# A two-layer model kernel on one core: gate sigmoids moved behind the softmax heads, norms four tiles at a time, and a re-ordered convolution

## The reference, cut to what matters

```
def conformer_conv(h, w_in, b_in, dw, dw_b, ln_g, ln_b, w_out, b_out):
    u = h @ w_in + b_in
    u = u[..., :D] * jax.nn.sigmoid(u[..., D:])
    u = causal_dwconv(u, dw) + dw_b            # 31 taps
    u = jax.nn.silu(layernorm(u, ln_g, ln_b))
    return u @ w_out + b_out

def hybrid_layer(...):
    h = rmsnorm_2(x, norm_mix_g)
    gq, gk, gv, gr, glr, fq, fk, fv, ff, g_gla, g_fox = jnp.split(h @ w_in, IN_OFFSETS, axis=-1)
    o_gla = gla_chunked(...)                   # 4 heads
    o_gla = rmsnorm_2(o_gla, ...) * jax.nn.silu(gr)
    fqh = rmsnorm_2(fq, ...); fkh = rmsnorm_2(fk, ...)
    o_fox = fox_attention(fqh, fkh, fv, log_f) # 8 heads, softmax
    y = jax.nn.sigmoid(g_gla + gate_b[0]) * (o_gla @ w_gla_branch) \
        + jax.nn.sigmoid(g_fox + gate_b[1]) * (o_fox @ w_fox_branch)
    x = x + y @ w_out
```

## Time and profile before

| what | us |
|---|---|
| median of 3 runs | 2668.36 (2668.05 to 2668.66) |
| the profiled execution | 2671.43 |
| its span, first to last instruction | 2669.6 |
| PE busy in the span | 2539.5 (95%) |
| DVE busy | 1345.3 (50%) |
| ACT busy | 1138.2 (43%) |
| POOL busy | 996.6 (37%) |

### The profile page before, as it was taken

One profiled execution on the slowest core, in us unless ns is written; L12 is line 12 of the kernel. 1 busy time (PEld: TensorE's weight loads), 2 busy tenths in 40 slices (PEclk: granted clock), 3 DMA queues, 4 the chain that ended last, 5 costly groups with the idle time before them and its releaser, 6 DMA issues.

```text
span 2669.6 us, 62382 instructions
## 1 busy us (share of the span) xinstructions
PE 2539.5 (95%) x25300; PEld 2385.7 (89%) x25300; DVE 1345.3 (50%) x2023; ACT 1138.2 (43%) x1656; POOL 996.6 (37%) x488
## 2 busy tenths in 40 slices
PE   7998998999999999998999999999998989999998
PEld 6787886997999999876979999999997659999998
DVE  7566555623477731897333777521162234455521
ACT  7844445543444333325433444332436432444422
POOL 3333220551444444334313444444332103444442
PEclk8899999999999999998999999999999899999999
DMA  4221001431222233223212222333221102222232
GB/s 144 79 64 49 1 3 64 142 131 40 90 91 92 90 112 126 81 67 119 79 48 81 93 93 92 107 103 110 86 88 56 32 0 80 95 94 94 94 103 72
DMA packets 62181, 219.44 MB, mean 82 GB/s; under 512 B 6752, under 2 KB 9184, under 8 KB 61408
## 3 DMA queue, kind: packets, MB, share of 16 engines
q1 hardware_dynamic: 58880, 207.76, 23.9%
q10 hardware_dynamic: 3168, 9.75, 1.0%
HBM read 213.29 MB, written 4.19 MB: 81 GB/s over the span
## 4 chain that ended last, share of the span: by engine, by line
PE 79%; DVE 9%; issue 7%; ACT 4%; POOL 2%; DMA 0%; DVEq 0%; POOLq 0%; ACTq 0%
PE psum L561 66%; DVE psum L2615 5%; PE psum L703 3%; PE psum L711 2%; POOL wl L510 2%; PE psum L1054 1%; PE psum L1011 1%; PE psum L1230 1%; PE psum L1229 1%; ACT wh L1356 1%; DVE psum L2205 0%; PE psum L1252 0%; DVE fox_max L2801 0%; PE psum L1264 0%; PE psum L673 0%
## 5 line engine op out<-in xcount | busy, mean ns | idle before, releaser
L510 POOL TENSOR_TENSOR wl<-raw,wh 128x1024 fp32r<-128x1024 f32 x388 | 950.5, 2459 | 1530.0 <-ACT wh L1356 1530.0
L561 PE MATMUL psum<-acth,wh 128*128 128x256 f32 x3792 | 764.9, 283 | 17.1 <-DVE actl L2211 6.5
L561 PE MATMUL psum<-actl,wh 128*128 128x256 f32 x3792 | 755.1, 281 | 0.0
L561 PE MATMUL psum<-acth,wl 128*128 128x256 f32 x3792 | 754.9, 280 | 0.0
L1356 ACT ACTIVATE wh<-raw 128x1024 fp32r<-128x1024 f32 x388 | 406.8, 1055 | 560.7 <-PE psum L561 545.8
L561 PEld LDWEIGHTS psum<-acth,wh 128*128 128x128 f32 x3792 | 583.9, 189 | 33.9 <-issue 26.5
L561 PEld LDWEIGHTS psum<-acth,wl 128*128 128x128 f32 x3792 | 583.0, 189 | 0.0
L561 PEld LDWEIGHTS psum<-actl,wh 128*128 128x128 f32 x3792 | 582.2, 189 | 0.0
L2545 DVE TENSOR_TENSOR cu<-psum,rstd 128x512 f32<-128x512 f32 x132 | 91.0, 690 | 241.8 <-PE psum L561 224.6
L561 PE MATMUL psum<-hidh,wl 128*128 128x256 f32 x1056 | 209.5, 276 | 0.0
L561 PE MATMUL psum<-hidh,wh 128*128 128x256 f32 x1056 | 209.4, 276 | 0.0
(11 more groups left out here) (434 smaller groups left out, 4094.2 us busy)
## 6 DMA issues: line engine op xcount, KB each, us to landing
raw<-in_weights SPq DMA_DIRECT2D x388, 512.0 KB, 3.4
xt<-in_x SPq DMA_DIRECT2D x4, 512.0 KB, 5.6
xt<-in_x ACTq DMA_DIRECT2D x1, 2048.0 KB, 9.0
out_x<-xt SPq DMA_DIRECT2D x6, 256.0 KB, 2.3
mem<-in_mem ACTq DMA_DIRECT2D x1, 1024.0 KB, 10.8
memn<-memh ACTq DMA_DIRECT2D x1, 1024.0 KB, 6.3
memn<-meml ACTq DMA_DIRECT2D x1, 1024.0 KB, 9.6
memh<-memn ACTq DMA_DIRECT2D x1, 1024.0 KB, 4.9
```

Source lines behind the costliest of these rows:

```text
L510: pool.tensor_tensor(wl[:, s, :], raw[:, s, :], wh[:, s, :].bitcast(F32), ALU.subtract).then_inc(split_done, 1)
L561: ins = pe.matmul(out[:, n:n + HALF], w, m[:, n:n + HALF], start=first and n == 0, stop=last and n + HALF >= out.shape[1])
```

## The change

In the convolution: `PETAPS` goes from 6 to 7; PE's taps go singly between the `cin` tiles; ACT loads the Sigmoid table ahead of the first sigmoid, which now comes before the diagonals; DVE runs the chains of tiles 5, 6 and 7 three abreast and then 6 and 7 together; the sum of squares goes from PE to DVE (eight adds into `rstd` and one matmul, `norm_total`), the four `kv1b` tiles stand together, the Ln table is loaded early, and two `weight_high` move behind the Silu loop.

In the hybrid: ACT's `gate(n)` only loads weights; all 16 sigmoids run in fox heads 5, 6 and 7; the fox norms go four tiles at a time, Ln and Exp in place in banks 4 to 7, where DVE reads them; gate tiles stand elsewhere between the norm sums, and `gate(10 + h)` comes right after gla head h. DVE's product with the gates waits for `gated`.

```
-PETAPS = 6
+PETAPS = 7
@@ PE, convolution
-                taps(2)
-                dense("cin", "norm_conv", acth, actl, units=4, skip=8)
-                taps(4)
-                dense("cin", "norm_conv", acth, actl, units=4, skip=12)
+                for k in range(2, 6):
+                    taps(k)
+                    for j in (4 + 2 * k, 5 + 2 * k):
+                        tile("cin", j, "norm_conv", acth, actl)
                 taps(6)
+                taps(7)
...
-                for j in range(2):
+                for j in range(4):
                     tile("kv1b", j, "norm_mem0", memh, meml, n=MEM)
-                norm_sum("ln")
-                for j in range(2, 4):
-                    tile("kv1b", j, "norm_mem0", memh, meml, n=MEM)
+                norm_total("ln")
@@ PE, hybrid
-                for j in range(0, 8, 2):
-                    fox_sum(j)
-                    fox_sum(j + 1)
-                    gate(5 + j // 2)
-                pe.wait_ge(frs_ready, 8)
+                fox_sum(0)
+                fox_sum(1)
+                gate(5)
+                fox_sum(2)
+                fox_sum(3)
+                gate(6)
+                gate(7)
+                for j in range(4, 8):
+                    fox_sum(j)
+                gate(8)
+                pe.wait_ge(fox_scaled, 5)
                 gla_scores(0)
                 gate(9)
+                pe.wait_ge(fox_scaled, 8)
                 for h in range(4):
                     gla_head(h)
+                    gate(10 + h)
                     if h < 3:
                         gla_scores(h + 1)
-                    gate(10 + h)
                     gla_sum(h)
@@ ACT, convolution
+                act.activation(tmp[:, 0, 0:1], b_eps, ACT.Sigmoid)
+                sigmoid(0)
+                weights(0)
                 diagonals(2)
...
+                act.activation(tmp[:, 0, 0:1], b_eps, ACT.Ln)
@@ ACT, hybrid
                 def gate(n):
-                    act.wait_ge(evacuated, t0 + 25 + n + 1 + UC)
-                    g_ = (gate_b if n // KT else gate_a)[:, n % KT, :]
-                    act.activation(g_, g_, ACT.Sigmoid, bias=pc("gate_b_2", n)).then_inc(gated, 1)
                     inner_high(25 + n, 26 + n)
+                def sigmoids(n0, n1):
+                    for n in range(n0, n1):
+                        g_ = (gate_b if n % 2 else gate_a)[:, n // 2, :]
+                        act.activation(g_, g_, ACT.Sigmoid, bias=pc("gate_b_2", n // 2 + KT * (n % 2))).then_inc(gated, 1)
...
                     act.activation(fpt[:, h % 2, 7 * P:10 * P], bank[2][:, 0:3 * P], ACT.Identity).then_inc(fpt_a, 1)
+                    if h == 7:
+                        sigmoids(12, 16)
...
+                    if h in (5, 6):
+                        act.wait_ge(evacuated, t0 + 41 + UC)
+                        sigmoids(6 * (h - 5), 6 * (h - 4))
@@ DVE, convolution
-                both(4, 11, 23, 6)
-                both(5, 17, 30, 12)
-                both(6, 18, 30, 13)
-                alone(7, 17, 12)
+                both(4, 13, 25, 7)
+                three(18, 30, 12)
+                both(6, 18, 18, 12)
...
+                for k in range(KT):
+                    if k + 2 < KT:
+                        centred(k + 2)
+                    dve.wait_ge(sq_ready, plan("ln", "sq") + k + 1)
+                    dve.wait_ge(sq_used, plan("ln", "sq") + k + SC)
+                    dve.tensor_tensor(rstd[:, :], rstd[:, :], sq[:, k % 2, :], add).then_inc(sq_used, 1)
```

More of the change, by code:

```diff
@@ L195, in build_program @@
             plan.take("kv1b", tile=4)
-            plan.take("ln", sq=KT, rstd=1, split=KT)
+            plan.take("ln", sq=KT, rstd=1, split=KT, total=1)
             plan.take("cout", tile=8, x=KT)
@@ L1069, in convolution, with taps @@
             def convolution():
[L1071 to L1081, removed]
+                def taps(k):
+                    pe.wait_ge(diag_ready, k - 1)
+                    pe.wait_ge(glu_ready, k + 1)
+                    if k >= 4:
+                        pe.wait_ge(u_ready, k - 3)
+                    for j in range(PETAPS):
+                        ins = pe.matmul(bank[4 + k % 4][:, :], diag[k % 2][:, j, :], gp[:, k, j:j + T],
+                                        start=(j == 0), stop=(j == PETAPS - 1))
+                    ins.then_inc(tap_mm, 1)
                 def mean(k0, k1):
@@ L1852, in gates, with weights, diagonals @@
                                    bias=pc("conv_b_in", k + KT)).then_inc(sig_ready, 1)
[L1854 to L1861, removed]
+                def weights(k):
+                    weight_high(UNIT0["cin"] + 2 * k + SLOTS)
+                    weight_high(UNIT0["cin"] + 2 * k + 1 + SLOTS)
+                def diagonals(k):
+                    if k >= 4:
+                        act.wait_ge(tap_mm, k - 3)
+                    for j in range(PETAPS):
+                        ins = act.activation(diag[k % 2][:, j, :], ident, ACT.Identity,
+                                             scale=pc("conv_dw", k * CONVW + j))
+                    ins.then_inc(diag_ready, 1)
                 def convolved(k):
@@ L1905, in convolution @@
                 act.activation(bank[5], rstd[:, :], ACT.Exp, scale=-0.5).then_inc(rstd_ready, 1)
-                for j in range(2, 4):
-                    kv_tile("kv1b", j, vals[:, 4 + j, :])
                 g0 = plan("ln", "split")
@@ L1914, in convolution @@
                     act.activation(acth[:, k, :], tmp[:, (g0 + k) % 2, :], ACT.Identity).then_inc(hi_ready, 1)
+                for j in range(2, 4):
+                    weight_high(UNIT0["kv1b"] + j + SLOTS)
                 deltas_normed("cout", 1, "norm_x1", h=headh)
@@ L2012, in hybrid @@
                 act.wait_ge(qk_ready, 1)
-                for j in range(0, 8, 2):
-                    gate(4 + j // 2)
-                    fox_rms(j)
-                    if j < 6:
-                        for s in range(2, 4):
-                            fox_square(j + s)
+                gate(4)
+                fox_square(2)
+                fox_square(3)
+                gate(5)
+                fox_square(4)
+                fox_square(5)
+                fox_rms(0)
+                gate(6)
+                gate(7)
+                fox_square(6)
+                fox_square(7)
+                fox_rms(4)
                 gate(8)
@@ L2634, in both, with three @@
                         tap(b, jb - i, 0 if ja - i == first_of(a) else 1)
+                def three(ja, jb, n):
+                    for k in (6, 7):
+                        dve.wait_ge(glu_ready, k + 1)
+                        dve.wait_ge(tap_mm, k - 1)
+                    for i in range(n):
+                        last = ja - i == first_of(5)
+                        tap(5, ja - i, 2 if i else 0)
+                        tap(6, jb - i, 1 if last or not i else 2)
+                        tap(7, jb - i, 1 if last else 2)
                 evac(0)
@@ L2763, in hybrid @@
                     chain.step(ins)
-                gate(4)
+                for n in range(4, 7):
+                    gate(n)
                 for j in range(8):
-                    if j and j % 2 == 0:
-                        gate(4 + j // 2)
+                    if j == 4:
+                        gate(7)
                     dve.wait_ge(frs_ready, j + 1)
```

94 lines of the change are left out of this document (54 added, 40 removed).

## The result

The changed kernel took, in the first comparison, 2654.33 us (median of 5 executions, 2647.91 to 2655.98), the kernel before 2668.66: a ratio of 0.994, 95% interval 0.9926 to 0.9953, or 14.3 us faster. The forecast was 18.6 faster, between the two, and 2650.

What follows compares the result with a forecast made beforehand. DVE's tap chain bounds the convolution; PE, waiting for ACT's norms, bounds the hybrid up to the fox scores. Convolution -14.4 and hybrid -4.2 (-17.5 + 13.3) give -18.6: median 2668.36 to 2649.8 us, range 2637 to 2663.

Steps and rivals of the forecast that it cites:

- Convolution, taps: DVE's chain in the convolution: earlier, shorter first product, fewer taps and fewer alone; last tap ends 8.4 us earlier, at 1227.9.
- the second product behind POOL: Convolution, DVE: the second product falls inside POOL's next run, at about 1085.2, and loses 1.0 us.
- The +0.8 for waits of the last scaling and sigmoid: Convolution: last scaling waits for PE's last cin tile, last sigmoid for ACT's weight copies; together 0.8 us lost.
- The eight adds of the squares: Convolution's norm, DVE: adds reading two SBUF operands might be held by POOL; nothing charged, at most 2.4 us once.
- PE keeps up: Convolution: PE's work sums to 120.9 us, ending at 1226.0 or 1229.5, just before DVE; mean ends 9.5 or 7.8 earlier.
- The norm: Convolution, mean to first Silu: adds and squares hide behind four kv1b tiles; 16.8 us instead of 21.8, so -4.9.
- Fox sums to fox scores: Hybrid: PE's waits for ACT's norms vanish, leaving PE's 82.6 us of full-clock work instead of 100.1: -17.5, bounds 12.5 and 17.5.
- Head 0: Hybrid, first fox head: PE's 3.75 us wait and the low clock after it remain; loss of 7 or 8 us kept.
- the rival of the cheaper second half: Hybrid: head 0's low clock shrinks by 7 us and the tail costs only 8.5; -30.4, 2638 us; chance 0.20.
- The tail: Hybrid, fox head 6 to branch: sigmoids make PE wait 7 and 3 us, both products then at low clock; +13.3 us.
- PE didn't become the convolution's bound: Rival, convolution: taps and tiles wait for each other, clock falls once; with a dearer tail -10.5, 2658 us; chance 0.13.
- the low clock of the tail did not reach `out2`: Rival, slower: PE's tail waits bring the low level into branch and out2; 2684 us at six tiles; chance 0.04.

Runs made afterwards that it cites:

- the spread kernel: Changed kernel with the gates' sigmoids four at a time in fox heads 1 to 4, behind the copies: 2641.34 us (ratio 0.9881), and again 2639.3 us (0.9882).
- the second profile: Profile of the changed kernel run again, with no edit, beside other experiments on the same chip: 2652.2 us, against 2672.99 before.
- the undone norm: Changed kernel with the convolution's norm put back: squares summed on PE in eight matmuls, kv tiles as before; 2660.0 us.
- the mean's fill: Kernel with sigmoids in fox heads 1 to 4 and head 0's wait filled, plus four unread matmuls in the wait within the convolution's mean: 2631.38 us, ratio 0.9852.
- the filled kernel: Kernel with sigmoids in fox heads 1 to 4, plus four unread matmuls in PE's wait ahead of head 0's transposes: 2635.24 us, ratio 0.9858.

## Why the prediction held, point by point

**Convolution, taps: -8.4 forecast, -8.9 measured.** The first product's start and length (-3.1 and -1.6) came as written. So did the second product behind POOL: 1.80 us for the 0.77 of its shape, +1.0. The last product was held the same way (1.44), which I had not seen, +0.7; nor had I seen that the fifth and sixth products before had been held too (1.11 and 0.82), -0.4 now. The taps gave -5.6, for 4.0 and 1.5 forecast, at 0.67 us each with three chains abreast. The +0.8 for waits of the last scaling and sigmoid did not come: DVE stands nowhere between the first product and the last tap. The forecast is good to half a microsecond because these small misses nearly cancel.

The eight adds of the squares, for which I named up to 2.4 us, cost nothing: each runs at 0.68 us, and POOL starts at 1239.76 only. On this the Trainium skill, "SBUF — State Buffer", "Who interferes with whom", says which operations to look at, those with two SBUF inputs while GpSimd reads SBUF; the traces agree: the slow products all began while POOL ran, and the first one, now begun before it, takes 0.75.

**PE keeps up: forecast by 2 us or less, measured 3.54.** From its first tap to the sixth tile of the mean PE took 118.85 us (1103.03 to 1221.88), 2.0 less than the lower of my two sums. What I left out was the price of being early: the low clock came with the wait, so the mean ended 8.0 us earlier (1229.04 - 1062.97 against 1239.11 - 1065.03) and not 9.5. Here the sum failed by 1.5. That the low clock was the reason is seen in the spread kernel's second profile, where it did not come: there the mean ended at 1226.89 - 1062.45, 9.6 earlier than before.

**The norm: -4.9 forecast, -4.8 measured**, and 4.6 when undone alone. The convolution gave 12.8 where 14.4 was forecast, and 14.1 to 14.5 in the three profiles without the low clock at the mean.

**Fox sums to fox scores: -17.5 forecast, -16.9 measured.** PE's floor of 82.6 us was 83.16, and the clock 1.00. The size was right, but it says nothing on the parts: I had named both, ACT's relief and the tile that now lies ahead of the scores, and priced neither alone. The runs show that either would have given most of it, the order 10.6 us and the sigmoids' removal 8.1, and that with the order there the removal, the costliest edit later, adds 2.9.

**Head 0: no change forecast, and so it was** in the second profile (18.35 against 18.09). The first profile's 12.98 is the shrinking that the rival of the cheaper second half counted with; of the twelve profiles here without a fill, before and after among them, two show it (12.98, and 12.96 where the sigmoids are left out), and ten 17.3 to 18.35. The changed kernel itself shows it once in two, so the change doesn't bring it about each time.

**The tail: +13.3 forecast, +11.1 measured.** The start of head 6's product, 5.2 us late by the forecast, was 8.11 us behind the transposes instead of 3.00, so 5.1. PE's waits were 6.8 and 4.1 us for the 7 and 3 written. The term that was too large is the products at the low clock: 4.31 and 3.38 us, not 4.8 each. The low level did not last through the second. In one other execution of the same code, under the undone norm, both took 4.6 and the tail 23.7, so +12.7. Into the branch the low clock reached 1.6 us deep, which I had named as a possible 2.

**The sum.** -12.8 - 16.9 + 11.1 + 1.6 = -17.0 from the stretches that the change touches, the forecast was -18.6, and the medians gave -14.3 and -20.8. Part of the nearness is luck: 1.6 too much at the convolution and 0.6 at the fox sums stand against 2.2 too much charged at the tail. What is left, 1.6, is the low clock in the branch, which I had named and not counted. The rest of the profile's -23.5 is head 0 (-5.1), and -2.1, +1.1 and -0.4 in stretches of the same code. In the 14 profiles the norm's first matmul, behind code that no kernel here changes, starts between 1061.2 and 1066.4 us: so much do executions differ, and a forecast cannot be told right or wrong below some 5 us by one execution.

None of the rivals came true as a whole: PE didn't become the convolution's bound, and the low clock of the tail did not reach `out2`.

## What to carry to other kernels

Before moving work off a busy stretch, change its order there: with a gate tile behind each head the engine that was late had time enough, and the move was worth 2.9 us in front for 11 behind. If work must be moved, look for a place where its engine stands in every round (here over 7 us ahead of each Exp) and not one where another engine waits for the next thing in its queue. And price a wait of PE with the low clock that can follow it: filling the wait of 3.5 us ahead of head 0 with matmuls that nobody reads took 1.5 to 7 us off head 0, some 6 as a rule, though the wait's own length stayed. Before a single profile is taken as the effect of an edit, look for the same stretch in the profiles without it: the mean's fill seemed to give 1.6 us, and three profiles without it show the same time.

## What the runs showed of the hardware that I had not expected

The low clock after a wait has no fixed length. Behind the same wait of 3.5 to 3.8 us the work from head 0's transposes to head 1's took 12.98 and 12.96 us in two executions and 17.3 to 18.35 in ten, at granted clocks between 0.87 and 0.53, and 11.44 with the wait filled. Behind the mean's wait of 3.5 us it did not come at all in three executions of eleven. The six waits of 1.2 us between the heads never brought it, and the one of 1.7 us in the last heads did once in nine profiles (product 4.61 us instead of 2.39). What decides its length, and why it came there in the filled kernel, stays open.

A load of a table costs ACT 1.28 us here and nothing besides: the sigmoid at 2159.06 starts 0.01 us behind the load that ends at 2159.05, and the load at 2112.91 in the spread kernel starts 0.02 us behind the sigmoid ahead of it. The Trainium skill, "ScalarE: Activation LUTs", "What ACT_TABLE_LOAD costs", counts 2.66 us for a switch with its drain. By an estimate from that figure the spread sigmoids, with two loads a head, would have needed 2.8 us more and used up the 1.96 to 2.65 us that ACT still stood; the trace shows the load's 1.28 alone.
